# Even layer's first attention: turned probabilities copied by ScalarE into two buffers instead of by VectorE into one

## The reference, cut to what matters

```python
def diff_attend(q, k, v, lam, scale):
    s = jnp.einsum('bqhcd,bkhcd->bhcqk', q, k).astype(jnp.float32) * scale
    p = jax.nn.softmax(s, axis=-1)
    w = (p[:, :, 0] - lam * p[:, :, 1]).astype(v.dtype)
    return jnp.einsum('bhqk,bkhd->bqhd', w, v)
```

## Time and profile before

| | us |
|---|---|
| median of 3 runs | 2408.7 |
| profiled execution, its own time | 2410.49 |
| its span, first to last instruction | 2409.2 |
| PE busy | 2173.4 (90%) |
| DVE busy | 921.2 (38%) |
| ACT busy | 562.2 (23%) |
| POOL busy | 261.3 (11%) |
| copies L910, both attentions | x40, 404 to 957 ns |
| this attention, first scores to last value product | 562.9 to 677 |

### The profile page before, as it was taken

How to read it: one execution, slowest core, us unless ns; L and a number is a source line. 1 busy time by engine, 2 the same in 40 slices (tenths; PEclk the granted TensorE clock), 3 DMA queues, 4 the chain that set the end, 5 groups by cost and what they waited for, 6 DMA issues and landing times.

```text
span 2409.2 us, 31887 instructions
## 1 busy us (share of the span) xinstructions
PE 2173.4 (90%) x13058; PEld 1144.7 (48%) x13058; DVE 921.2 (38%) x2313; ACT 562.2 (23%) x1216; POOL 261.3 (11%) x544
## 2 busy tenths in 40 slices
PE   5999999998888997999999999889999697787777
PEld 3896544456667443444444444456664232222222
DVE  4467545347875132221222123666651411111111
ACT  3244432114555020000000001455540100000000
POOL 0001000001134110000000000432211000000000
PEclk8999999999999998999999999899999899989999
DMA  8225600111000349999999998100024999999998
GB/s 274 88 71 181 239 24 16 70 53 36 1 1 1 141 195 383 406 397 391 392 401 399 390 397 321 37 1 1 3 104 176 344 406 398 404 408 407 402 412 342
DMA packets 103502, 548.74 MB, mean 228 GB/s; under 512 B 7967, under 2 KB 23087, under 8 KB 74430
## 3 DMA queue, kind: packets, MB, share of 16 engines
q1 hardware_dynamic: 94942, 519.97, 54.6%
q0 software_dynamic: 6144, 20.98, 3.6%
q10 hardware_dynamic: 2272, 5.77, 0.6%
HBM read 525.72 MB, written 20.97 MB: 227 GB/s over the span
## 4 chain that ended last, share of the span: by engine, by line
PE 71%; DMA 16%; DVE 6%; ACT 2%; issue 2%; POOL 1%; SPq 1%; another core or an unknown queue 0%; DVEq 0%; ACTq 0%; POOLq 0%
PE PS L2308 14%; DMA AR<-in_w_exp_up_dram 8%; PE PS L1886 8%; PE PS L2321 7%; PE PS L1075 6%; PE PS L766 5%; PE PS L2454 5%; DMA AR<-in_w_exp_down_dram 4%; PE PS L785 3%; PE PS L987 3%; DMA AR<-in_w_exp_gate_dram 2%; PE PS L450 2%; PE PS L808 1%; PE PS L1547 1%; DMA AR<-in_w_ada_dram 1%
## 5 line engine op out<-in xcount | busy, mean ns | idle before, releaser
L2454 PE MATMUL PS<-AR 128*64 128x512 f32 x1536 | 373.3, 635 | 83.7 <-DMA AR<-in_w_exp_gate_dram 43.0
L2308 PE MATMUL PS<-AR 128*64 128x512 f32 x1536 | 343.8, 600 | 3.0 <-DVE AR L2380 2.0
L2454 PEld LDWEIGHTS PS<-AR 128*64 128x64 f32 x1536 | 115.4, 144 | 316.5 <-issue 255.6
L2308 PEld LDWEIGHTS PS<-AR 128*64 128x64 f32 x1536 | 106.8, 138 | 215.0 <-issue 214.9
L1886 PE MATMUL PS<-AR 128*128 128x512 f32 (+1 forms) x480 | 189.4, 550 | 0.7 <-ACT AR L670 0.7
L766 PE MATMUL PS<-AR 96*128 96x512 f32 (+3 forms) x480 | 184.2, 501 | 2.3 <-POOL AR L743 0.9
L2321 PE MATMUL PS<-AR 128*32 128x256 f32 x3072 | 175.7, 380 | 0.0
L873 DVE TENSOR_REDUCE AR<-PS 128x1 f32<-128x768 f32 (+1 forms) x160 | 135.8, 849 | 98.9 <-PE PS L766 79.1
L828 ACT ACTIVATE AR<-PS,AR 128x768 f32<-128x768 f32 (+1 forms) x160 | 130.4, 815 | 57.2 <-DVE AR L873 26.4
L1075 PE MATMUL PS<-AR 128*128 128x512 f32 x320 | 139.8, 599 | 1.0 <-DVE AR L1098 0.6
L2321 PEld LDWEIGHTS PS<-AR 128*32 128x32 f32 x3072 | 94.9, 110 | 76.6 <-issue 15.7
(11 more groups left out here) (387 smaller groups left out, 2869.5 us busy)
## 6 DMA issues: line engine op xcount, KB each, us to landing
AR<-in_w_exp_gate_dram SPq DMA_DIRECT2D x64, 2048.0 KB, 18.3
AR<-in_w_exp_up_dram SPq DMA_DIRECT2D x64, 2048.0 KB, 23.2
AR<-in_w_exp_down_dram SPq DMA_DIRECT2D x63, 2048.0 KB, 19.6
AR<-in_w_ada_dram SPq DMA_DIRECT2D x30, 2048.0 KB, 12.0
AR<-in_w_in_dram SPq DMA_DIRECT2D x12, 1024.0 KB, 5.1
AR<-in_w_in_even_dram SPq DMA_DIRECT2D x4, 2048.0 KB, 8.3
AR<-in_w_out_dram SPq DMA_DIRECT2D x2, 2048.0 KB
AR<-in_w_out_even_dram SPq DMA_DIRECT2D x2, 2048.0 KB, 7.7
```

The costliest lines, as they stand in the source:

```text
L2308: t = pe.matmul(bank(b)[64 * q_:64 * q_ + 64, :], op, w[:, c, 512 * q_:512 * q_ + 512], start=(h == 0 and c == 0), stop=(h == 1 and c == 3 ...
L2454: m = pe.matmul(bank(b)[64 * q_:64 * q_ + 64, :], op, w[:, c, 512 * q_:512 * q_ + 512], start=(h == 0 and c == 0), stop=(h == 1 and c == 3 ...
```

## The change

For an attention with A.mixed the copy of the turned matrix moves from DVE's program to ACT's, at the same step, behind the exp of that step. The buffer index becomes (i // 2) % 2, so successive pairs use the two buffers in turn, and the copy waits for the value products of the pair before the last (i - 4) rather than of the last (i - 2). For the other attention of these functions nothing changes.

```diff
+        def turned(A, i):
+            return A.Pt[(i // 2 if A.mixed else i) % len(A.Pt)]
@@ pe_attn
-                    ptc = A.Pt[i % len(A.Pt)]
+                    ptc = turned(A, i)
@@ act_attn
-                if 0 <= i < n and i % 2 == 0 and not A.units[i].get("skip"):
+                if 0 <= i < n and i % 2 == A.mixed and not A.units[i].get("skip"):
                     nk = A.units[i]["nk"]
-                    if i >= len(A.Pt):
-                        S.wait_ge("full", "pv", A.tag, i - len(A.Pt))
+                    k = i - (2 if A.mixed else 1) * len(A.Pt)
+                    if k >= 0:
+                        S.wait_ge("full", "pv", A.tag, k)
                     S.wait_ge("full", "tr", A.tag, i)
-                    s.copy(A.Pt[i % len(A.Pt)][:, 0:nk], psf[:, turn_at(A, i):turn_at(A, i) + nk]).then_inc(*S.read("tr", A.tag, i))
+                    s.copy(turned(A, i)[:, 0:nk], psf[:, turn_at(A, i):turn_at(A, i) + nk]).then_inc(*S.read("tr", A.tag, i))
@@ dve_attn
-                if 0 <= i < n and i % 2 and not A.units[i].get("skip"):
+                if 0 <= i < n and i % 2 and not A.mixed:
                     nk = A.units[i]["nk"]
-                    k = i - (len(A.Pt) if not A.mixed else 2 * len(A.Pt))
-                    if not A.mixed and i >= len(A.Pt):
+                    if i >= len(A.Pt):
                         V.wait_ge("full", "pv", A.tag, i - len(A.Pt))
-                    if A.mixed and i >= 2:
-                        V.wait_ge("full", "pv", A.tag, i - 2)
                     V.wait_ge("full", "tr", A.tag, i)
                     v.tensor_copy(A.Pt[i % len(A.Pt)][:, 0:nk], psf[:, turn_at(A, i):turn_at(A, i) + nk])\
```

## The result

The change made the kernel slower by about half of what was forecast. In 15 runs each, taken in turn, the changed kernel has a median of 2415.22 us (2413.0 to 2420.66) and the kernel before 2411.02 (2405.7 to 2414.65); the ratio is 1.0022, 95% interval 1.0015 to 1.0029, so +5.3 us of 2411. Forecast were +10.8 us and 2419.5 for a median of 2408.7. The profiled execution has a span of 2413.5 us, 4.3 more than before.

The account below looks back on a forecast made before the run. PE was taken to bound the regular pair, with DVE's copy just in time. Terms 11.9 - 1.8 + 0 + 0.7 = 10.8 us on the profiled 2410.49 gave 2421.3; with the median 1.8 lower, 2419.5, range 2413.5 to 2427.

Parts of the forecast that it names:

- The loop: Regular 768-key pairs: ACT's copy behind the exp delays the value products 0.79 us, pair 5.73 for 4.94; 15 pairs, +11.9 us.
- The hand-over of the copy to PE: Between the end of ACT's copy and PE's value products in 768-key pairs: 0.05 us, part of the 0.79 delay.
- The pairs with fill: Three 768-key pairs with DVE's fill subtractions ahead of the maximum: each gives back 0.6 us, 1.8 in all.
- Sixteenth pair: Last 768-key pair, its copy beside a 256-key exp: taken as 0 us, bounds -0.2 and +0.8.
- 256 keys: Pairs with 256 keys: value products 0.44 us later, mostly covered by PE's wait; +0.7 us, bounds 0 and 3.5.
- The attention as a whole: Sum of the forecast's terms over this attention: +10.8 us.
- Second buffer and DVE's relief: In this attention: DVE's freed time and the dropped wait for the value products of i - 2, both costed at nothing.
- mostly hidden: Rival: part of the 0.79 us is covered, or fills give all 3.3 back; total 6 to 7 us, 2415; chance 0.12.
- So a delay goes through to the end.: Behind the attention: no load is under way in between, so the attention's whole delay reaches the kernel's end.
- The rival in my text that a clock could fall: Rival: PE, with more idle time in the loop, falls to 1.2 GHz; 5 pairs +12 us, 2432; chance 0.1.

Follow-up runs that it names:

- ACT copies, one buffer: Changed kernel with one buffer again: ACT copies behind the exp, waiting for the value products of i - 2; ratio to the kernel before 1.0038, then 1.0018.
- ACT, products later: Changed kernel with value products and output copy one pair later, five steps behind the scores instead of three; ratio to the kernel before 0.9973, then 0.9965.
- DVE, products later: Kernel before with two buffers, DVE still copying, and value products and output copy one pair later; ratio to the kernel before 0.9982.
- ACT, products later, fill later: Changed kernel with later value products, plus DVE's fill subtractions one step later, behind the odd unit's maximum; 2398.72 us, ratio to the kernel before 0.9953.

## Why the prediction was half right

**The loop, right.** Copy behind the accumulator read by 0.09 us (591.47 to 591.56), duration 0.79 (forecast 0.80), pair 5.78 (5.73), PE's wait 0.97 (0.90). The hand-over of the copy to PE is 592.50 - 592.35 = 0.15 us, not 0.05, which makes the difference; DVE's copies had 0.14 before. The 0.05 of the earlier trace rows was the wrong one to take. Why it is shorter there isn't shown: PE starts with a weight load in both. Reordering and doubling the copy (above) show that order and duration are the cause.

**The pairs with fill, mis-sized.** Three gave back 1.8 us in the forecast. The fill pairs are 5.91, 6.18 and 5.92, or 0.13, 0.40 and 0.14 above regular ones, where before they were 1.11, 1.36 and 1.12 above 4.93. They gave back 2.9 us. I had the exp of the even unit follow the scaling by 0.94 us, its recorded length; it follows by 0.84, and the casts and subtractions move up:

```profile
598.02 0.94 ACT L843 ACTIVATE AR<-AR 128x768 f32<-128x768 f32 x1
...
598.86 0.90 ACT L831 ACTIVATE AR<-PS,AR 128x768 f32<-128x768 f32 x1
```

**Sixteenth pair and 256 keys, small misses.** The step to the sixteenth value products is 3.97 us instead of 4.52, where I took 0 and had -0.2 as the bound. The eight pairs after it take 24.7 us instead of 24.3 in the first two traces, and 23.7 instead of 24.4 in the second two, where I took +0.7. The first trace of the changed kernel has one of these pairs in the slow clock (L811 with 1.20 instead of 0.68 us), which is what I had priced; the second has none.

**The attention as a whole, right.** +9.4 us in the first trace, and 121.7 against 113.2, or +8.5, in the second pair of traces; forecast +10.8. The loop gave a little more than forecast (0.84 a pair for 0.79), the fill and the last pairs a little less.

**Second buffer and DVE's relief, right.** Neither moves anything by itself.

**The rival "mostly hidden", right in its number only.** It named 2415 us, which is what was measured. Its reason didn't come true: it wanted part of the 0.79 covered in the loop, or fills that give back everything at the lower price. The pair grew by 0.84, and the attention by 8.5 to 9.4.

**What failed: "So a delay goes through to the end."** Here the prediction lacked a term: it looked only at loads, and put the clock behind the attention at nothing. The stretches behind the attention, from starts in the traces, in us; the clock is the mean granted one of the first stretch:

| kernel | last value products to output projection | its clock | from there to first expert product | last value products to end |
|---|---|---|---|---|
| before | 112.8, 112.7 | 0.94, 0.94 | 141.3, 140.7 | 1733.4, 1735.0 |
| DVE copies, two buffers | 112.7 | 0.94 | 141.2 | 1732.1 |
| changed | 109.6, 109.7 | 0.98, 0.98 | 138.9, 139.2 | 1728.1, 1729.3 |
| ACT copies, one buffer | 111.8, 112.1 | 0.94, 0.94 | 140.8, 141.2 | 1733.3, 1732.7 |
| ACT, products later | 109.5, 110.3 | 1.00, 0.99 | 138.9, 139.0 | 1728.2, 1728.5 |
| DVE, products later | 113.5 | 0.94 | 141.1 | 1736.9 |
| ACT's copy ahead of the exp | 113.1 | 0.93 | 138.3 | 1730.6 |
| ACT, products later, fill later | 111.4 | 0.97 | 139.7 | 1735.6 |
| ACT's copy twice | 109.5 | 0.98 | 138.9 | 1727.3 |

The program behind the attention is the same in all. In the changed kernel it is 5.3 and 5.7 us shorter than in the two traces of before: 3 us up to the output projection, 2 behind. The granted clock (the number before the DMA share; two windows, at the start of the second attention and around the start of the output projection) shows where, first before:

```profile
675.00:690.00 15.00, 13.02 (x86) 10.79 (x86) 9.76 (x16) 7.43 (x14) 3.54 (x10) 0.84 0.00 1
777.00:795.00 18.00, 14.18 (x48) 8.44 (x47) 2.88 (x9) 3.23 (x5) 0.29 (x1) 0.62 0.33 113
```

then after, where the second place lies 6 us later:

```profile
777.00:795.00 18.00, 13.03 (x95) 9.03 (x93) 7.70 (x24) 7.95 (x22) 4.30 (x13) 0.91 0.00 1
787.00:793.00 6.00, 4.43 (x26) 3.34 (x26) 1.32 (x4) 1.64 (x4) 0.00 (x0) 0.72 0.00 0
```

and the repeat of before, and the repeat of after:

```profile
777.00:795.00 18.00, 14.05 (x52) 8.44 (x53) 3.00 (x9) 3.78 (x8) 0.29 (x1) 0.62 0.30 102
```

```profile
777.00:804.00 27.00, 21.61 (x116) 12.40 (x113) 8.09 (x25) 7.76 (x20) 5.37 (x13) 1.00 0.38 133
```

Before, TensorE ran at 1.2 GHz through most of the 15 us from the end of the second attention (from 780 to 788.6 us PE stands idle for 2.5 of 8.6 us, between small tiles) into the output projection, in both traces. After, it ran so for 3 to 4 us in one and not at all in the other. The output projection keeps PE busy without a gap (84.67 of 84.70 us from 788.6 before), so each us at half clock there costs nearly half a us; its longest product in those first us takes 1.22 us in both traces of before and 0.67 in both of the changed kernel, and the median is 0.59 in all four. The later products alone have no such stretch either (clock 1.00 from 768 to 795 us in their repeat), and 109.5 to 110.3 us. The whole stretch up to the output projection, first in the kernel before and then with the later products, has the same work of DVE, ACT and POOL, and PE alone is longer in it:

```profile
675.82:788.62 112.80, 100.03 (x884) 82.28 (x884) 73.16 (x143) 61.67 (x132) 40.52 (x112) 0.94 0.01 1
```

```profile
669.84:779.29 109.45, 95.87 (x891) 79.12 (x889) 73.43 (x144) 62.03 (x133) 40.69 (x112) 1.00 0.01 1
```

The traces are ordered by the clock of this stretch: 109.5 to 110.3 us at 0.98 to 1.00, 111.4 at 0.97, 111.8 to 113.5 at 0.93 and 0.94. They are not ordered by the attention: a form with the changed kernel's attention to 0.1 us, the one-buffer one, has it (clock 0.75 from 777 to 804) and takes 2.3 us longer up to the output projection.

So the traces show that the return comes from where the half clock falls, and that the kernel before has it twice in the same place. I had written that were it so, the half clock would belong to the program's own timing; but the one-buffer form, with the same timing in the attention, falls on the other side twice, and what puts it there is not settled.

The timed runs have the changed kernel at +5.3 and +7.0 us (0.0022 and 0.0029 of 2411), against +8.5 to +9.4 in the attention, and the one-buffer form at +9.2 and +4.3. Of these runs only the mean granted clock of the whole run is on record, and for the kernel before not in the first comparison. In the comparison with both forms it is 0.9641 before (29 runs), 0.9663 for the changed kernel (12) and 0.9675 for the one-buffer form (11); in the one before that, 0.9647 before (26) and 0.9664 for the one-buffer form (5). So the clock was higher in both forms than in the kernel before, which is the sign of the return. Among runs of one kernel in one comparison a clock higher by 0.001 goes with 0.7 us less (164 runs, correlation -0.64). My estimate from these numbers is 1.5 us back for the changed kernel, and 1.2 and 2.4 us for the one-buffer form where it had +9.2 and +4.3. The order is that of the times, so the swap of the two forms goes with the clock too, but the estimate covers only a part of it. Where in a timed run the clock was low isn't on record, so for the timed runs the cause is likely and not shown.

The rival in my text that a clock could fall had it inside the attention; it stayed at 1.00 through the 768-key part, and the effect was behind it and of the other sign.

## What to carry to other kernels

Ask of a moved instruction what stands ahead of it in its new engine's program, not how idle that engine is: ACT was idle for 1.6 us of each pair, but ahead of the exp, while the copy stood behind it. A second buffer brought nothing until the consumer was moved a round later; then the copy cost nothing that could be seen in either place that was tried, on either engine. Work that is slipped in (fill) did best behind the operation that the next round waits for. And a delay of a few us in one stage need not reach the end: look at the granted clock of the stages behind it, before and after.

## What the runs showed of the hardware that I had not expected

A PSUM copy of 128x768 takes 0.79 us on ScalarE and 0.94 on VectorE (x16 each), one of 256 columns 0.36 against 0.42 (x8 each). Of two ScalarE instructions in a row the second starts about 0.1 us before the recorded end of the first, the scaling and the exp too (598.02 + 0.94 to 598.86). And the kernel before has its stretches at 1.2 GHz from 655 to 800 us in the same places in two traces taken on different occasions, to about a us, while the changed kernel's two traces differ in them (clock 0.91 and 1.00 in the windows above), and the one-buffer form, whose attention takes as long, has them elsewhere again.
